# Differential attention units threaded through the query and value projections, in a two-layer fp32 decoder trunk

## What is computed

```python
kv = rmsnorm(x, kv_norm_g) @ kv_w            # 2048 columns: keys (1024), values (1024)
k = partial_rope(kv[..., :1024]);  v = kv[..., 1024:]
q = partial_rope(rmsnorm(x, g) @ w_q)        # 8 heads x 2 x 64
s = einsum('bqhcd,bkhcd->bhcqk', q, k) * scale
p = masked_softmax(s, kpos <= t)
a = p[:, :, 0] - lam * p[:, :, 1]            # lam from diff_lambda
o = einsum('bhqk,bkhd->bqhd', a, v)          # 8 heads x 128
o = rmsnorm(o, subln_g) * (1.0 - lam_init)
x = x + o.reshape(B, S, 1024) @ w_out
```

## Time and profile before

| | |
|---|---|
| median of three runs | 644.7 us |
| profiled execution, its time | 644.81 us |
| its span in the trace | 643.0 us |
| PE busy | 628.3 us (98%) |
| DVE busy | 528.1 us (82%) |
| ACT busy | 418.6 us (65%) |
| DMA | 110.16 MB, 171 GB/s mean |
| chain that ended last, share of PE | 88% |

### The profile page before, as it was taken

One profiled execution on the slowest core, in us unless ns is written; L12 is line 12 of the kernel. 1 busy time (PEld: TensorE's weight loads), 2 busy tenths in 40 slices (PEclk: granted clock), 3 DMA queues, 4 the chain that ended last, 5 costly groups with the idle time before them and its releaser, 6 DMA issues.

```text
span 643.0 us, 10694 instructions
## 1 busy us (share of the span) xinstructions
PE 628.3 (98%) x3596; PEld 527.6 (82%) x3596; DVE 528.1 (82%) x953; ACT 418.6 (65%) x818; POOL 36.3 (6%) x87
## 2 busy tenths in 40 slices
PE   9999989999999999999999999989999999999995
PEld 8998666779888888888888888768988888888894
DVE  5687697867998889988888556877899889888887
ACT  6755468748666666666667464884866666666666
POOL 0000023300000000000012000150000000000000
PEclk9999999999999999999999999989999999999998
DMA  8967040035565555555516644603455555555521
GB/s 324 333 241 278 12 186 3 1 131 169 176 233 183 183 184 190 190 195 196 197 65 203 214 173 176 251 2 131 163 198 198 196 196 196 192 187 181 190 69 66
DMA packets 21744, 110.16 MB, mean 171 GB/s; under 512 B 2640, under 2 KB 3024, under 8 KB 12752
## 3 DMA queue, kind: packets, MB, share of 16 engines
q1 hardware_dynamic: 21424, 109.53, 47.5%
q10 hardware_dynamic: 288, 0.22, 0.1%
HBM read 108.68 MB, written 1.05 MB: 171 GB/s over the span
## 4 chain that ended last, share of the span: by engine, by line
PE 88%; DVE 8%; ACT 2%; issue 1%; DVEq 0%; ACTq 0%
PE psU L678 21%; PE psA L469 13%; PE psA L470 13%; PE psA L471 13%; PE psU L683 10%; PE psU L894 2%; PE psA L854 1%; PE psU L879 1%; PE psA L795 1%; DVE arena L1822 1%; DVE arena L2115 1%; PE psU L658 1%; PE psU L657 1%; PE psU L656 1%; DVE win_lo L1703 1%
## 5 line engine op out<-in xcount | busy, mean ns | idle before, releaser
L678 PE MATMUL psU<-hA,win_hi 128*128 128x512 f32 x608 | 190.8, 395 | 0.0
L683 PEld LDWEIGHTS psU<-hA,win_lo 128*128 128x128 f32 x608 | 114.2, 188 | 26.6
L683 PE MATMUL psU<-hA,win_lo 128*128 128x256 f32 x608 | 119.4, 278 | 0.0
L1796 DVE TENSOR_TENSOR win_lo<-stage,win_hi 128x1024 fp32r<-128x1024 f32 x86 | 104.9, 1221 | 0.0
L678 PEld LDWEIGHTS psU<-hA,win_hi 128*128 128x128 f32 x608 | 95.3, 189 | 2.8
L1289 ACT ACTIVATE win_hi<-stage 128x1024 fp32r<-128x1024 f32 x89 | 93.3, 1050 | 5.6 <-PE psA L471 5.6
L1822 DVE SCALAR_TENSOR_TENSOR arena<-arena,prm 128x255 f32<-128x255 f32 (+1 forms) x168 | 77.3, 481 | 3.7 <-ACT arena L1301 0.7
L1703 DVE TENSOR_TENSOR win_lo<-stage,win_hi 128x1024 fp32r<-128x1024 f32 (+3 forms) x50 | 55.8, 1152 | 13.4 <-ACT win_hi L1212 13.3
L469 PE MATMUL psA<-wout_hi,act_hi 128*128 128x512 f32 x168 | 65.9, 392 | 0.3
L470 PE MATMUL psA<-wout_lo,act_hi 128*128 128x512 f32 x168 | 65.5, 390 | 0.0
L471 PE MATMUL psA<-wout_hi,act_lo 128*128 128x512 f32 x168 | 65.4, 389 | 0.0
(11 more groups left out here) (319 smaller groups left out, 1128.9 us busy)
## 6 DMA issues: line engine op xcount, KB each, us to landing
stage<-in_w_ffn_in SPq DMA_DIRECT2D x44, 1024.0 KB, 4.8
stage_out<-in_w_ffn_out SPq DMA_DIRECT2D x44, 516.0 KB, 5.0
stage<-in_w_kv SPq DMA_DIRECT2D x8, 1024.0 KB, 4.8
stage<-in_w_dq SPq DMA_DIRECT2D x4, 1024.0 KB, 4.9
stage<-in_w_dout SPq DMA_DIRECT2D x4, 1024.0 KB, 4.8
stage<-in_w_group SPq DMA_DIRECT2D x3, 1024.0 KB, 5.2
stage<-in_w_nsa_out SPq DMA_DIRECT2D x3, 1024.0 KB, 4.8
stage<-in_w_phi SPq DMA_DIRECT2D x2, 1024.0 KB, 6.0
```

What stands on the lines that cost most here:

```text
L678: mm(o, win_hi[:, slot, cs], hA[:, k, :, :].rearrange("p a q -> p (a q)"), start=k == 0, stop=False)
L683: last = mm(o[:, 0:S], win_lo[:, slot, cs], hA_hi[:, k2, :], start=False, stop=k2 == KT - 1)
L1796: last = dve.tensor_tensor(win_lo[:, win, cs], stage[:, slot, cs], win_hi[:, win, cs].bitcast(F32), sub)
```

## The change

The eight units are spread over the projections. `project` takes a function `at`, which it calls ahead of each of the eight 128-row slices of a pair of chunks (slices 0 to 3 are the first chunk, 4 to 7 the second). The key transposes stand in chunk 5, the query transposes and scores of units 0 and 1 in chunks 6 and 7, and units 0 to 6 follow in chunks 8 to 11, with the value products of units 0 to 3. Behind chunk 11 are left the exponentials of unit 7, its transposes, and the products of units 4 to 7, which stand between the matmuls of out 0.

All scores lie in `psU` now, by u % 2, and wait for the copy of the turned probabilities of unit u - 2. `aT` has eight places, and ACT alone copies to it. Out 0 is loaded into `stage_out` and out 1 into `phi_k1` (`d_out0`, `d_out1`), both early, on a semaphore `side_in`; out 0 is split between chunks 6 and 7. DVE and ACT get new orders; POOL does the head norm of units 0 to 3 in one pass, ahead of its half of the low part of out 1. The core of the diff:

```diff
+C_SIDE = C_DO + 1
+D_OUT_AT = C_KV + 7
+def place_of(s):
+    if s == C_DO:
+        return D_OUT_AT
+    return s + 1 if D_OUT_AT <= s < C_DO else s
@@ SP
+                if s in (C_DO + 2, C_DO + 3):
+                    prev_s = s - 4
             for i in range(N_KV + N_DQ):
                 load_main(C_KV + i, a_dq[i - 4] if 4 <= i < 8 else a_kv[i if i < 4 else i - N_DQ], W)
-            for i in range(N_DO):
+                if i == 4:
+                    sp.wait_ge(sem["out_lo"], NJ)
+                    sp.dma_start(d_out0, a_do[0]).then_inc(sem["side_in"], 16)
+                if i == 9:
+                    sp.wait_ge(sem["in_lo"], place_of(C_DO) + 1)
+                    sp.dma_start(d_out1[:, :], a_do[1]).then_inc(sem["side_in"], 16)
+            for i in range(2, N_DO):
@@ PE
+                        if at is not None:
+                            at(kk)
+            def in_q0(kk):
+                if kk == 4:
+                    dk_transposes()
+            def in_q1(kk):
+                if kk == 3:
+                    dq_first()
+                if kk == 4:
+                    diff_scores(0)
+                if kk == 5:
+                    diff_scores(1)
+            def in_v0(kk):
+                if kk == 1:
+                    diff_transpose(0)
+                if kk == 2:
+                    diff_scores(2)
+                    diff_transpose(1)
+                    dq_second()
+                if kk == 3:
+                    diff_scores(3)
+                if kk == 4:
+                    diff_transpose(2)
+                if kk == 6:
+                    diff_scores(4)
+            def in_v1(kk):
+                if kk == 0:
+                    diff_transpose(3)
+                if kk == 2:
+                    diff_transpose(4)
+                    diff_scores(5)
+                    diff_pv(0)
+                    diff_pv(1)
+                if kk == 3:
+                    diff_scores(6)
+                    diff_pv(2)
+                    diff_pv(3)
+                if kk == 5:
+                    diff_transpose(5)
+                if kk == 6:
+                    diff_transpose(6)
+                    diff_scores(7)
             heads_T(0)
-            diff_pv(ND - 1)
-            out_project(C_DO, hB_hi, hB_lo, 2 * KVH * TT, 1, 3, next_heads)
+            diff_pv(4)
+            diff_pv(5)
+            d_out(0, 0)
+            diff_transpose(7)
+            diff_pv(6)
+            heads_T(1)
+            diff_pv(7)
+            pe_.wait_ge(sem["do_ready"], 2 * 6)
+            d_out(0, 1)
+            d_out(1, 0)
+            d_out(1, 1, (0,))
+            heads_T(2)
+            d_out(1, 1, (1,))
+            out_project(C_DO, hB_hi, hB_lo, 2 * KVH * TT, 1, 3, lambda c: heads_T(3), range(2, 4))
@@ ACT, behind chunk 11
             heads_hi(0)
-            for u in range(4, ND):
-                head_squares(u)
+            d_exps(7)
+            out_heads(4)
+            out_heads(5)
+            head_squares(4)
+            head_squares(5)
+            copy_aT(7)
             split(C_DO + 2)
             heads_hi(1)
+            head_squares(6)
+            head_squares(7)
@@ DVE, behind chunk 11
+            heads_lo(0)
             mix_probs(7)
-            copy_aT(7)
-            dve.wait_ge(sem["do_ready"], 2 * (ND - 2))
+            split(C_DO + 1, (0,))
             out_heads(ND - 2)
-            heads_lo(0)
+            heads_lo(1)
             out_heads(ND - 1)
-            dve.wait_ge(sem["in_lo"], C_DO + 2)
-            split(C_DO + 2)
-            heads_lo(1)
             heads_rstd(dve, 4, 4, "sub1_step", "sub1_rstd")
             scale_heads(dve, 2, "sub1_scaled")
             scale_heads(dve, 3, "sub1_scaled")
+            dve.wait_ge(sem["in_lo"], C_DO + 2)
+            split(C_DO + 2)
```

More of the change, by code:

```diff
@@ L483, in xT_part, with project @@
                         last.then_inc(sem["xT_bank"], 1)
-            def project(s0, h_hi, h_lo, out, width, k_tiles, h_waits=None, between=None):
+            def project(s0, h_hi, h_lo, out, width, k_tiles, h_waits=None, between=None, at=None):
                 for half in range(2):
@@ L1002, in _, with head_pairs_T @@
             ffn(0, C_F0)
+            ND = DH // 2 * TT
+            def head_pairs_T(bank, src, i):
+                for mi in range(2):
+                    for t in range(TT):
+                        last = pe_.transpose(bank[:, (mi * TT + t) * P:(mi * TT + t + 1) * P],
+                                             src[:, t, 2 * (2 * i + mi):2 * (2 * i + mi) + 2, :].rearrange("p h d -> p (h d)"), ident[:, :])
+                return last
             def dk_transposes():
@@ L1050, in diff_scores @@
                 last.then_inc(sem["dscores"], 1)
[L1052 to L1064, removed]
             def diff_transpose(u):
@@ new lines, in _ @@
+            for g in range(6):
+                if g >= 2:
+                    pe_.wait_ge(sem["proj_act"], NG + g - 1)
+                    pe_.wait_ge(sem["proj_dve"], NG + g - 1)
+                if g == 5:
+                    pe_.wait_ge(sem["dq_act"], 2)
+                    pe_.wait_ge(sem["dq_dve"], 2)
+                hh, hl = (hB_hi, hB_lo) if g in (2, 3) else (hA_hi, hA_lo)
+                project(C_KV + 2 * g, hh, hl, [psA[:, 2 * (g % 2) + t, :] for t in range(TT)], 512, 4,
+                        {0: 2 * KT, 2: 3 * KT}.get(g), None, {2: in_q0, 3: in_q1, 4: in_v0, 5: in_v1}.get(g))
@@ L1594, in _ @@
                     last.then_inc(sem["proj_act"], 1)
-                if c == 6:
+                if c == 0:
+                    h_hi(hB_hi, O_AG + KT, 2, 2 * KT, range(KT // 2, KT))
+                if 2 <= c < 6:
+                    split(C_KV + c + 2)
+                if c == 4:
                     for i in range(0, 4, 2):
@@ L1657, in _ @@
-            head_squares(2)
-            head_squares(3)
+                    split(C_DO)
+                if c == 6:
+                    q_copy(0)
+                    split(C_KV + 8)
+                    d_exps(0)
+                    d_exps(1)
+                if c == 7:
+                    copy_aT(0)
+                    split(C_KV + 9)
+                    copy_aT(1)
+                if c == 8:
+                    q_copy(1)
+                    d_exps(2)
+                    split(C_KV + 10)
+                    copy_aT(2)
+                    d_exps(3)
+                    d_exps(4)
@@ new lines, in _ @@
+                if c == 9:
+                    copy_aT(3)
+                    split(C_KV + 11)
+                    copy_aT(4)
+                if c == 10:
+                    out_heads(0)
+                    out_heads(1)
+                    head_squares(0)
+                    head_squares(1)
+                    d_exps(5)
+                    out_heads(2)
+                    out_heads(3)
+                    head_squares(2)
+                    head_squares(3)
+                    d_exps(6)
+                    copy_aT(5)
+                    split(C_DO + 1)
+                    copy_aT(6)
@@ L2233, in _ @@
                         dve.tensor_scalar(vals[:, 0, (g - 4) * 512:(g - 3) * 512], psA[:, 2 * (g % 2), :], rstd[:, 0:1], None, ALU.mult).then_inc(sem["proj_dve"], 1)
-                if c == 6:
+                if c == 0:
+                    h_lo(hB_lo, hB_hi, O_AG + KT, range(KT // 2, KT))
+                if 2 <= c < 6:
+                    split(C_KV + c + 2)
+                if c == 4:
                     for i in range(1, 4, 2):
@@ L2237, in _ @@
                         dve.tensor_copy(keysT[:, i * 512:(i + 1) * 512], free_banks[i]).then_inc(sem["dk_dve"], 1)
-                if c == 10:
+                    split(C_DO)
                     dve.wait_ge(sem["lam_exp"], 1)
```

261 lines of the change are left out of this document (119 added, 142 removed).

## The result

The kernel after takes 645.92 us (median of 7 runs, 645.32 to 647.11); the kernel before took 643.33 us beside it (7 runs, 642.98 to 644.87). The ratio is 1.0033, with a 95% interval of 1.0023 to 1.0043, that is 1.5 to 2.8 us slower. The forecast was 647.4 us, 2.7 above its 644.7 for the kernel before; of the 1.5 us between 647.4 and 645.9, 1.4 are that the median of the kernel before, over seven runs, is 643.3.

A forecast was written before the change was run, and what follows sets the result against it. PE, busy for 98% of the span, was taken as the bound. From 644.81 us profiled, + 1.0 for out 3's later start and + 1.7 for the clock gave 647.5, or 647.4 at the median; range over all 641.8 to 649.4.

The forecast's parts named there:

- The mechanism: Out 2's low part behind the head norm delays F0's load; ACT, then PE wait 4.0 us before out 3; clock falls.
- PE up to out 2: PE's new order from chunk 4 to out 2: out 2 starts at 438.5, 3.3 us earlier than before.
- the 0.4 charged: PE's wait ahead of unit 4's value product, for the value copies of chunk 11: 0.4 us.
- The steps of 0.09: Steps where PE switches between unit pieces and projection or output matmuls: 1.1 us added for about ten places.
- The load of F0: Issued at 438.5 after out 2's low part, 4.1 us later than before; lands 443.3, so out 3 starts at 448.7.
- The clock: Clock falls to half after PE's wait ahead of out 3: 1.7 us charged, bounds 0 and 2.7.
- another fall: Clock fall at 427.0 in the kernel before: half speed for 3.4 us, doing the work of 1.7.
- The sum: Whole kernel: 644.81 us profiled, + 1.0 for out 3's later start, + 1.7 for the clock; 647.4 at the median.
- A in full: Rival: no wait for F0 ahead of out 3, clock full, out 3 at 444.7: 641.8 us; chance 0.17.
- B: Rival: the wait ahead of out 3 comes but the clock holds: 645.8 us; chance 0.16.
- C: Rival: DVE bounds the projections, from chunk 8's low part with 0.4 us of slack: 649.0 us; chance 0.08.
- D: Rival: units leave their chain late, PE waits between chunks 8 and 11: about 648 us; chance 0.04.

The follow-up runs named there:

- e1: Kernel after with, on DVE, the low part of out 2 back ahead of heads_lo(1): 639.61 us, ratio to the kernel before 0.9928.
- e4: Kernel after with out 3 and heads 6 and 7 ahead of F0's first half on ACT and DVE: 639.91 us, ratio to before 0.9937.
- e3: Kernel before with only the low part of out 2 moved behind the head norm on DVE: 649.77 us, ratio to before 1.0096.
- e2: Kernel after with 17 unused matmuls of 512 columns between out 2 and out 3: 644.08 us, ratio to before 1.0001.
- e7: Kernel after with 8 unused matmuls of 512 columns between out 2 and out 3: 643.94 us, ratio to before 1.001.
- e6: Kernel before with out 3 and heads 6 and 7 ahead of F0's first half on ACT and DVE: 644.21 us, ratio 1.0003.

## Why the prediction was right, and where its sizes were off

The mechanism was the forecast's, with its steps in the order given. Two sizes were off in opposite directions, so that the sum (0.9 too high by the table) is nearer than the larger of them; that much is luck.

**PE up to out 2.** Forecast 80.4 us (from 358.14 to 438.5), measured 78.89, so 1.5 too long. The waits were longer than the 0.4 charged: 0.50 ahead of the value product of unit 4, as said, 0.33 at `heads_T(1)` and 0.22 at out 2, 1.05 in all. The steps of 0.09 are there too. PE around the query transposes and the scores of unit 0:

```profile
374.02 1.03 PE L1045 MATMUL psU<-ident,tokB 128*128 128x128 f32 x8
374.81 0.47 PE L502 MATMUL psA<-win_hi,hB_hi 128*128 128x512 f32 x1
375.12 0.40 PE L503 MATMUL psA<-win_lo,hB_hi 128*128 128x512 f32 x1
...
376.37 0.71 PE L1089 MATMUL psU<-keysT,qrT 64*128 64x128 f32 x8
...
377.17 0.48 PE L502 MATMUL psA<-win_hi,hB_hi 128*128 128x512 f32 x1
```

From 374.81 to 375.12 are 0.31 where 0.23 is usual, and an even unit's scores cost 0.80 and the two steps, as charged. Too dear were the short pieces. The transposes of keys and queries I had charged with the duration of their row, 1.91 us, which reaches to the last result; by the distance of starts sixteen cost 1.67 in the kernel before (374.57 to 376.24). The others I had read from the tail, where each row also holds steps and small delays: an odd value product costs 0.82 and not 0.99, an odd unit's transposes 0.43 and not 0.53, a `heads_T` 0.36 and not 0.53, the eight query transposes at 374.02 0.79 and not 0.95. PE at two of these places:

```profile
420.68 1.06 PE L1123 MATMUL psA<-vals,arena 128*128 128x128 f32 x8
421.50 0.47 PE L502 MATMUL psA<-wout_hi,hB_hi 128*128 128x512 f32 x1
...
424.33 0.60 PE L1102 MATMUL psU<-ident,arena 128*128 128x128 f32 x4
424.76 0.61 PE L1123 MATMUL psU<-vals,arena 128*128 128x128 f32 x4
...
433.90 0.60 PE L1191 MATMUL psU<-ident,tokB 128*128 128x128 f32 x4
434.26 0.48 PE L502 MATMUL psA<-win_hi,hB_hi 128*128 128x512 f32 x1
```

Two transposes of an even unit between projection matmuls cost 0.13 and not 0.36 (393.56 to 393.69). Added up over the whole trace, all these pieces with their steps cost 22.8 us, where 24.3 and another 1.1 of steps were charged: 2.6 too much. Against that stand the waits (1.05 for 0.4) and the ten chunks (54.9 for 54.6, at 0.229 a matmul), which makes 1.6, and 1.5 is measured. The early loads of outs 0 and 1 took 7.4 and 6.8 us to land, not 4.8, and PE waited for neither.

**The load of F0.** Forecast: issued with the end of the low part of out 2, 80.4 us behind chunk 4. Measured 78.8 (436.00 less 357.23). It is early by as much as PE is, since the chain hangs on unit 7's transposes (at 424.33 on PE) over the copy of its turned probabilities, the high part of out 2, `heads_hi(1)` and `heads_lo(1)`, as the forecast had it. From the issue to out 3 the forecast was 10.2 us, measured 10.17. ACT's wait is 4.65, PE's 3.89 where 4.0 was said. This part, on which the sign rested, was right to 0.1 us, and e1, e4 and e3 show it from three sides.

**The clock.** Charged 1.7, measured 2.45 from out 3 to the end, inside the bounds of 0 and 2.7. This term was mis-sized: I took the loss of another fall, 3.4 us at 1.2 GHz, and here it lasted until 5.2 us of out 3 had passed. Nor was that other fall worth the 1.7: out 2 came only 1.0 us sooner without it (e3). The bound, half of out 3's 5.5 us, was the nearer value. That the clock belongs to the sum at all is shown by e2 and e7. In the Trainium skill, "TensorE: Matmul & The Clock Gate", section "What's actually happening", the low clock is the default and activity releases it, and the pair of the kernel after and e2 (2.4 us between them behind out 3) agrees.

**The sum.** - 4.79 + 4.15 + 2.45 = + 1.8, forecast + 2.7: the two sizes, 1.5 too dear and 0.75 too cheap. Of the rivals, A in full needed, with PE as early as it came, the load to land before 436.7 (out 3 could have begun at 436.12 + 5.9 = 442.0, and 5.35 us of work lie between landing and out 3); it landed at 440.8. e1 is that case made by hand, and at 639.6 it is 2.2 us faster than the 641.8 that I gave it: 1.7 are PE's sum (78.65 for 80.4) and 0.2 lie between out 2 and out 3 (5.96 where 6.2 was charged). B, no fall of the clock, is what e7 shows: 643.9. For C and D the profile has nothing: the first of PE's waits behind chunk 4 is that at 420.17, behind chunk 11, and the low part of chunk 8, with its 0.4 us of slack, was in time.

What stays open: by the ratio of the runs the change costs 2.1 us (1.5 to 2.8), by one pair of profiled executions 1.8, and the starts of chunk 4 lie 1.0 us apart from execution to execution. What makes them differ is not shown, nor in how many executions of the kernel before the clock falls at 427. Of 23 of them, the 14 with a mean granted clock of 0.993 or 0.994 have a median of 644.2 us, the nine with 0.996 or more 643.3, which would fit a fall in the first and none in the others.

## What to carry to other kernels

When a stretch is made shorter, look for the instruction that frees a buffer for what comes after it, and see that it was not moved behind something long: here a subtraction of 2.35 us, put behind a head norm, turned a gain of 4.8 us into a loss of 1.8, and two lines moved back made it a gain of 4.6. Where an engine takes work in order, what waits for a transfer belongs behind what does not (e4), which costs nothing where there is slack (e6). And a wait on PE is to be charged with what the clock takes after it, which was more than half of the wait in the kernel after (2.45 of 3.89 us) and nothing behind the 2.30 us in the trace of e7.

## What the runs showed of the hardware

Whether the clock falls is not settled by the work alone. In the kernel before PE is busy for 3.28 us of the 6.00 up to 427.0, and the clock falls for 3.4 us. In e3, where the same units stand in the same order, PE has the same waits there (1.22 us in the longest), and the clock stays at 1.00. In e6, the same again up to there, it falls 68.2 us behind chunk 4, where it was 68.9 in the kernel before. Between the traces of the kernel before and e3 this fall made 1.0 us.

How long the low clock lasts differs much from case to case. PE idled 3.89 us in one piece in the kernel after; the clock fell some 2.3 us into it and stayed at 0.50 for 6.8 us, which cost 2.45 us. In e3 PE idled 4.87 us, the clock was at 1.00 until the last of it and low for some 3.4 us from 451.0, which cost 1.7. In e7 2.30 us of idle time left it at 1.00. So a longer wait was followed by the smaller loss; what decides it these runs do not show. A load of 1 MB on SP's queue landed in 4.8 us in the kernel after and in 6.5 in e3: its windows have the DMA engines at a share of 0.90 from 440 to 441, and at 0.20 and 0.06 in the last two us, a tail of few bytes for which ACT waited.

```profile
440.00:441.00 1.00, 1.00 (x7) 0.81 (x6) 0.94 (x1) 0.00 (x0) 0.00 (x0) 1.00 0.90 205
...
443.00:444.00 1.00, 1.00 (x8) 0.87 (x7) 0.00 (x0) 0.00 (x0) 0.00 (x0) 1.00 0.20 82
444.00:445.00 1.00, 1.00 (x6) 0.84 (x5) 0.00 (x0) 0.00 (x0) 0.00 (x0) 1.00 0.06 25
```
